# A four-layer fp32 network on one core: five and three tile places, halved opening and ending, and one rounding moved

## The reference

```python
for i in range(2):   # block one
    u = rms_norm(h, g_mix_pre);  gq, gk, gv, gg, ra, aq, ak, av, ga, gb = split(u @ w_in)
    mixed = sigmoid(ga) * (gla(...) @ w_o_gla) + sigmoid(gb) * (attention(...) @ w_o_attn)
    h = h + rms_norm(mixed @ w_out, g_mix_post)
    g, up = split(rms_norm(h, g_ffn_pre) @ w_ffn_in)
    h = h + rms_norm((silu(g) * up) @ w_ffn_out, g_ffn_post)
    h = h + rms_norm(sigmoid(h @ w_ple_gate) * (p @ w_ple_proj), g_ple_post)
for i in range(2):   # block two
    x = x + 0.5 * swiglu(rms_norm(x), ffn1)
    x = x + merged(recurrent, attention) @ w_o
    x = x + 0.5 * swiglu(rms_norm(x), ffn2)
    x = x + sigmoid(rms_norm(x) @ ple_w_gate + b) * (p @ ple_w_proj)
return rms_norm(x, final_norm)
```

## Time and profile before

| | us |
|---|---|
| median of the runs (3) | 2286.14 |
| the profiled execution | 2287.08 |
| its span, first to last instruction | 2285.3 |
| PE busy / DVE busy / ACT busy | 2260.3 / 1577.3 / 1317.1 |
| granted TensorE clock over the span | 0.998 |

### The profile page before, as it was taken

How to read it: one execution, slowest core, us unless ns; L and a number is a source line. 1 busy time by engine, 2 the same in 40 slices (tenths; PEclk the granted TensorE clock), 3 DMA queues, 4 the chain that set the end, 5 groups by cost and what they waited for, 6 DMA issues and landing times.

```text
span 2285.3 us, 31183 instructions
## 1 busy us (share of the span) xinstructions
PE 2260.3 (99%) x13072; PEld 1985.0 (87%) x13072; DVE 1577.3 (69%) x1803; ACT 1317.1 (58%) x1797; POOL 39.0 (2%) x74
## 2 busy tenths in 40 slices
PE   8999999999999999999999999999999999999998
PEld 8898888878988888888898889888888898989886
DVE  6866767478766775667577767675776588667755
ACT  6665655477655655565448745554554558555544
POOL 1000000010000000010000000000100000000000
PEclk9999999999999999999999999999999999999999
DMA  7615555556245655566555355555665655455553
GB/s 227 227 65 184 185 193 188 183 189 231 96 148 184 203 185 193 184 203 193 184 181 178 119 191 191 196 187 186 200 208 177 202 167 166 142 191 183 186 193 120
DMA packets 323515, 411.92 MB, mean 180 GB/s; under 512 B 11600, under 2 KB 245456, under 8 KB 323376
## 3 DMA queue, kind: packets, MB, share of 16 engines
q1 hardware_dynamic: 318160, 394.68, 52.5%
q0 software_dynamic: 4928, 14.26, 2.1%
q10 hardware_dynamic: 288, 0.99, 0.1%
HBM read 408.85 MB, written 1.05 MB: 179 GB/s over the span
## 4 chain that ended last, share of the span: by engine, by line
PE 88%; DVE 5%; ACT 4%; DMA 1%; issue 1%; SPq 0%; DVEq 0%; ACTq 0%
PE banks L610 27%; PE banks L618 14%; PE banks L687 9%; PE banks L689 9%; PE banks L688 9%; PE banks L594 3%; PE banks L595 3%; PE banks L596 3%; DVE lo L1769 2%; ACT hi L1185 1%; DMA raw<-in_w_in 1%; PE banks L738 1%; PE banks L864 1%; PE banks L873 1%; PE banks L841 1%
## 5 line engine op out<-in xcount | busy, mean ns | idle before, releaser
L1769 DVE TENSOR_TENSOR lo<-raw,hi 128x2048 fp32r<-128x2048 f32 (+1 forms) x382 | 858.4, 2250 | 521.9 <-ACT hi L1185 518.0
L1185 ACT ACTIVATE hi<-raw 128x2048 fp32r<-128x2048 f32 (+1 forms) x382 | 715.7, 1878 | 254.3 <-DMA raw<-in_ffn_w_out 84.5
L610 PE MATMUL banks<-x_in,hi 128*128 128x512 f32 x2304 | 537.7, 390 | 0.0
L610 PEld LDWEIGHTS banks<-x_in,hi 128*128 128x128 f32 x2304 | 427.7, 188 | 86.1 <-issue 0.4
L618 PEld LDWEIGHTS banks<-x_in,lo 128*128 128x128 f32 x2304 | 286.5, 192 | 5.8 <-issue 0.2
L618 PE MATMUL banks<-x_in,lo 128*128 128x256 f32 x2304 | 289.3, 283 | 0.0
L594 PE MATMUL banks<-x_in,hi 128*128 128x256 f32 x736 | 210.5, 286 | 0.0
L595 PE MATMUL banks<-x_in,hi 128*128 128x256 f32 x736 | 208.2, 283 | 0.0
L596 PE MATMUL banks<-x_in,lo 128*128 128x256 f32 x736 | 208.2, 283 | 0.0
L687 PE MATMUL banks<-hi,x_hid 128*128 128x512 f32 x528 | 206.0, 390 | 0.0
L689 PE MATMUL banks<-hi,x_hid 128*128 128x512 f32 x528 | 205.5, 389 | 0.0
(11 more groups left out here) (343 smaller groups left out, 3081.0 us busy)
## 6 DMA issues: line engine op xcount, KB each, us to landing
raw<-in_w_in SPq DMA_DIRECT2D x108, 1024.0 KB, 5.1
raw<-in_ffn_w_in SPq DMA_DIRECT2D x88, 1024.0 KB, 5.1
raw<-in_w_ffn_in SPq DMA_DIRECT2D x44, 1024.0 KB, 5.1
raw<-in_ffn_w_out SPq DMA_DIRECT2D x40, 1024.0 KB, 5.1
raw<-in_w_ffn_out SPq DMA_DIRECT2D x20, 1024.0 KB, 5.1
raw<-in_w_o_gla SPq DMA_DIRECT2D x8, 1024.0 KB, 5.2
raw<-in_w_o_attn SPq DMA_DIRECT2D x8, 1024.0 KB, 5.2
raw<-in_w_out SPq DMA_DIRECT2D x8, 1024.0 KB, 5.1
```

What stands on the lines that cost most here:

```text
L610: mm = pe.matmul(bank[b + f], wh[:, k, f * P:(f + 1) * P], x[:, k, :, :].rearrange("p n s -> p (n s)"), start=(start and k == 0), stop=(k ...
L1185: act_fn(high, of, ACT.Copy).then_inc(hi_done.up(), 1)
L1769: tt(rest, of, parts(tile, hi)[0].bitcast(F32), ALU.subtract).then_inc(lo_done.up(), 1)
```

## The change

There are now five places of `raw`/`lo` and three of `hi`. The load of tile n waits for tile n-5, and ScalarE's rounding of tile n gets a wait of its own, for `tile_used` of tile n-3. The first tile is loaded, rounded and subtracted in two halves, the second rounded and subtracted in halves; `opening_rows` takes the place of `rows_in_turn` there and of 40 idle transposes. In the last layer the second 128 tokens of the last projection are done in two column halves, with a chain of halves behind them; the final root is a power on GpSimd, and the output leaves in three DMAs. Four orders differ: block one pumps to `pg[3]` ahead of `turned_high(x_a, 1, 1, 7)`; block two's `pg` stage moves one rounding behind the gates on ScalarE and one behind two `turned_low` on VectorE; VectorE rounds one tile later at `fl`.

```diff
-SLOTS = 4
+SLOTS, HIGHS = 5, 3
@@ pump, ScalarE
                     act.wait_ge(*landed(tile))
+                    if place(tile) >= HIGHS:
+                        act.wait_ge(*tile_used.at(tile.index + 1 - HIGHS))
@@ block one, ScalarE
                 turned_high(x_a, 1, 0, 6)
-                pump(pg[2].index)
+                pump(pg[3].index)
                 turned_high(x_a, 1, 1, 7)
@@ block two, ScalarE, pg
+                pump(pg[3].index)
+                act.wait_ge(*tile_used.at(pg[1].index + 1))
+                for t in range(T):
+                    gate(t, 0)
                 pump(pg[3].index + 1)
-                act.wait_ge(*tile_used.at(pg[1].index + 1))
-                for t in range(T):
-                    gate(t, 0)
@@ block two, VectorE, fl
-                used(BY2["fl"][0])
+                pump(BY2["fl"][0].index + 1)
+                dve.wait_ge(*tile_used.at(BY2["fl"][0].index + 1))
                 tt(fz[:], bank[0][:, 0:S], root_row[:], ALU.mult).then_inc(scaled.up(), 1)
...
+                pump(BY2["fl"][0].index + 2)
@@ block two, VectorE, pg
+                turned_low(x_in, *by_features[0])
+                turned_low(x_in, *by_features[1])
                 pump(pg[3].index + 2)
-                if not last:
-                    turned_low(x_in, *by_features[0])
-                    turned_low(x_in, *by_features[1])
@@ opening, SyncE, ScalarE, TensorE
+                if layer == 0 and tile == TILES1[0]:
+                    sync.dma_start(dst[:, 0:2, :], src[:, 0:2, tile.c0:tile.c0 + tile.nc]).then_inc(first_in.up(), 16)
+                    sync.dma_start(dst[:, 2:4, :],
+                                   src[:, 2:4, tile.c0:tile.c0 + tile.nc]).then_inc(raw_in[slot(tile)].up(), 16)
+                    return
+            first, second = TILES1[:AHEAD]
+            act.wait_ge(*first_in.at(1))
+            high_half(first, 0)
+            turned_high(x_in, *high_turns[0])
+            act.wait_ge(*landed(first))
+            high_half(first, 1)
+            turned_high(x_in, *high_turns[1])
+            act.wait_ge(*x_loaded[0].at(1))
+            norm_tile(0)
+            act.wait_ge(*landed(second))
+            high_half(second, 0)
+            high_half(second, 1)
...
-            idle_turns(40)
-            rows_in_turn(BY1["gva"], x_in, (0, 1), 0, (), *high_turns[2:])
+            opening_rows(BY1["gva"], x_in, (0, 1), *high_turns[2:])
@@ ending, VectorE
+                    ts(xn[:, 0, :], xn[:, 0, :], lroot[:, 0:1], None, ALU.mult).then_inc(xf_ready.up(), 1)
+                    dve.wait_ge(*tile_used.at(pg[3].index + 1))
+                    late_before(1)
+                    dve.wait_ge(*dve_step.now())
+                    late_added(0)
+                    late_times(1)
...
+                    for n in range(2):
+                        cut = slice(n * 512, (n + 1) * 512)
+                        ts(xn[:, 1, cut], xn[:, 1, cut], lroot[:, 1:2], None, ALU.mult).then_inc(xf_ready.up(), 1)
```

More of the change, by code:

```diff
@@ L408, in slot, with high_slot @@
             return place(tile) % SLOTS
+        def high_slot(tile):
+            return place(tile) % HIGHS
         def landed(tile):
@@ L1407, in _, with high_half @@
             warm(ACT.Sqrt)
[L1408 to L1414, removed]
+            def high_half(tile, n):
+                cut = slice(n * TILE // 2, (n + 1) * TILE // 2)
+                act_fn(hi[high_slot(tile)][:, cut], raw[slot(tile)][:, cut],
+                       ACT.Copy).then_inc((hi_done if n else first_hi).up(), 1)
+            first, second = TILES1[:AHEAD]
[10 more added lines that the diff above has]
+            high_half(second, 1)
             act.dma_start(cst[:, P:C_END], dram["consts"][:, P:C_END]).then_inc(const_in.up(), 16)
+            turned_high(x_in, *high_turns[2])
+            turned_high(x_in, *high_turns[3])
+            act.wait_ge(*x_loaded[1].at(1))
+            norm_tile(1)
             for layer in range(DEPTH):
@@ L1728, in _ @@
                     gate(t, 0)
+                pump(pg[3].index + 1)
                 for t in range(T):
@@ L1743, in _ @@
                 for t in range(T):
-                    if t or not last:
-                        act.wait_ge(*h_ready.next())
-                        square(h[:, t, 512:D], hsum[:, t, 1:2])
+                    act.wait_ge(*h_ready.next())
+                    square(h[:, t, 512:D], hsum[:, t, 1:2])
                     root(t, hsum, hbias)
-                    if not last:
-                        turned_high(x_in, *by_features[2 + t])
+                    turned_high(x_in, *by_features[2 + t])
         @block.vector
@@ L1975, in _, with low_half @@
             dve.sem_inc(layer_done.sem, 1)
-            layer_tiles[0] = TILES1[:AHEAD]
-            dve.wait_ge(*first_row.at(1))
[L1978 to L1984, removed]
+            def low_half(tile, n):
+                cut = slice(n * TILE // 2, (n + 1) * TILE // 2)
+                dve.wait_ge(*(hi_done.at(tile.index + 1) if n else first_hi.at(tile.index + 1)))
+                low(lo[slot(tile)][:, cut], raw[slot(tile)][:, cut], hi[high_slot(tile)][:, cut],
+                    lo_done if n else first_lo)
+            first, second = TILES1[:AHEAD]
+            dve.wait_ge(*first_row.at(1))
+            dve.wait_ge(*x_loaded[0].at(1))
+            for n in range(2):
+                with_gain(0, 0, n)
+            low_half(first, 0)
+            turned_low(x_in, *high_turns[0])
+            dve.wait_ge(*x_loaded[1].at(1))
+            with_gain(0, 1, 0)
+            low_half(first, 1)
+            turned_low(x_in, *high_turns[1])
+            with_gain(0, 1, 1)
+            low_half(second, 0)
+            low_half(second, 1)
+            turned_low(x_in, *high_turns[2])
+            turned_low(x_in, *high_turns[3])
             row_served(xn_ready)
@@ L2461, in _ @@
[L2461 to L2464, removed]
+                    gated(t, 1)
+                turned_low(x_in, *by_features[2])
+                turned_low(x_in, *by_features[3])
+                row_served(xn_ready)
+                invert_both()
+                nc.vector.memset(tick[:, 1:2], 0.0).then_inc(layer_done.up(), 1)
         return signals
```

162 lines of the change are left out of this document (127 added, 35 removed).

## The result

| | before | after |
|---|---|---|
| median, us | 2285.70 | 2305.43 |
| span of the profiled execution | 2285.3 | 2303.6 |
| PE busy | 2260.3 | 2264.1 |
| granted TensorE clock over the span | 0.998 | 0.996 |

Both medians are of four executions. The ratio is 1.0087 (95% interval 1.0074 to 1.0099): 19.7 us slower, where 19.9 had been forecast; the two profiled spans differ by 18.3. The four executions of the changed kernel reach from 2302.3 to 2307.3.

The account below looks back on a forecast made before the run. PE, busy 99% of the span, bounds the kernel; -4.2 + 6.6 + 5.5 + 5.8 - 0.1 + 6 + 0.3 = +19.9 on the profiled 2287.08 gives 2307.0, or 2306 beside the median. Range 2291 to 2314.

Parts of the forecast that it names:

- opening: First two tiles: halved loads and roundings let PE finish both at 23.6 instead of 27.8, -4.2 us (bounds 2.5 to 5 gained).
- block one, `pg`, two layers: `ffn1_out` into `pg`: copies of x_a wait behind delayed roundings, PE 0.5 and 2.8 us late per layer, +6.6 in all.
- `va`, two layers: Block two, `ffn1_out` into `va`: rounding of va[1] waits, the last piece comes 2.75 us late per layer, +5.5 in all.
- `ffn2_in`, two layers: Block two, `wo` into `ffn2_in`: rounding 3.6 us later, PE's transpose in by_halves 2.9 late per layer, +5.8 in all.
- the clock: Six new stalls of 2.2 to 2.9 us: five falls to 1.2 GHz at 1.2 each, +6 us (bounds 0 and 10).
- small terms and `pg` stage: `e` 0.4, `wo` of block one 0.6, `fl` -0.6, next transition -0.5, block two's `pg` stage nothing: -0.1 us together.
- ending: After the last matmul: halves and a dropped table load against a later VectorE queue, +0.3 us (bounds -1.5 and +1.5).
- `fl`: At the `fl` tile PE's 1.0 us of waiting should go, but ScalarE's sigmoids and logarithms are late next: 0.6 gained.
- the first rival: The stalls at the new waits leave TensorE's clock alone, so the time is 2300 us; chance 0.22.
- the rival of the lost opening: Without the idle transposes PE has gaps, falls to 1.2 GHz in the first tile, gives the gain back: 2310; chance 0.10.
- the wait moves and nothing is won: Block two's `pg` stage: the moved pump takes the 1.8 us wait from its place, but `xn` comes no earlier; 0 us.
- 1 us later from the site before: Ending: the whole `pg` stage on VectorE runs an estimated 1 us later because of the preceding site.

Follow-up runs that it names:

- covered: The changed kernel with idle transposes put into TensorE's stalls at six places: 2299.84 us, ratio 1.0064 to the kernel before.
- e2: The changed kernel with block one's call as before, pump(pg[2].index) ahead of turned_high(x_a, 1, 1, 7): 2298.03 us, ratio 1.0057.
- e3: The changed kernel with block two's norm_after copying two pieces before its pump and residual adding the last rows before its own: 2286.86 us, ratio 1.0006.
- e6: The kernel before with the halved opening and halved ending alone, four and four places, all four old orders: 2281.15 us, ratio 0.9981.
- e9: The mended orders with four and four places, but ScalarE's order in block two's `pg` stage as in the kernel before: 2283.05 us, one execution.
- e5: The kernel before with five places of raw and three of hi alone; opening, ending and orders as before: 2302.79 us, ratio 1.0073.
- the mended one: The changed kernel, five and three places, with block one's call back at pg[2] and copies first in both blocks: 2280.11 us, ratio 0.9975.
- e4: The changed kernel with 20, 16 and 20 idle transposes ahead of block one's fourth quarter, va[0] and ffn2_in's turned piece: 2299.84 us, ratio 1.0064.
- e1: The changed kernel with four places of raw and four of hi, everything else of the change kept: 2280.84 us, ratio 0.9983.
- e7: The changed kernel, five and three places, with e2's and e3's edits and the first x_a copy ahead of pg[1]'s rounding: 2280.11 us, ratio 0.9975.

## Why the prediction was right, point by point

| term | forecast | measured | from |
|---|---|---|---|
| opening | -4.2 | -3.7 | table, 28 us |
| block one, `pg`, two layers | +6.6 | +7.0 | steps to 474 and to 949 |
| `va`, two layers | +5.5 | +5.7 | 2.8 at 1160, 2.9 at 1813, covered |
| `ffn2_in`, two layers | +5.8 | +5.9 | 3.0 and 2.8 (from 9.91 at 2064), covered |
| the clock | +6 | +5.5 | last row, after less covered |
| small terms and `pg` stage | -0.1 | -1.6 | the rest |
| ending | +0.3 | -0.5 | spans |
| sum | +19.9 | +18.3 | |

"The rest" is 18.8 + 3.7 - 7.0 - 5.7 - 5.9 - 5.5 = -1.6, up to the last row of the table. By the column "covered" it holds -2.0 at the `pg` stage of block two, +0.5 twice at `e` (forecast 0.4 for the two), -0.4 at each of the two places behind block one's `pg` (515 and 970; forecast -0.5 for the two), -0.4 at `fl`, and +0.2 twice elsewhere (up to 935 and up to 2064).

That the sum came so near is in part luck. The terms are off by +0.5 (opening), +0.4 (block one), +0.3 (`va` and `ffn2_in`), -0.5 (clock), -1.5 (small terms) and -0.8 (ending), and these add up to only -1.6. The difference of the medians is nearer still (19.7) because the profiled execution of before, 2287.08, from which the forecast started, was 1.4 above its median.

**The three places.** Each step went as the forecast said, to 0.15 us: 0.61 at the first quarter (forecast 0.5), 2.8 at the fourth (2.8), 2.33 late at `va[0]` (2.2) and 2.8 at the piece behind it (2.75), 3.0 and 2.8 in `ffn2_in` (2.9). What made this possible is that the time of use of every tile can be read from SP's issues in the trace of before, and everything behind the waiting instruction was counted in its queue's order. e2 and e3 took them away one kind at a time, and the gain was what the forecast had put on them or more.

**The clock.** The sum is about right (5.5 for 6), its make-up is not: five falls at 1.2 were taken, there were four new ones at a mean of 1.4, and the old one went. The falls do not go by the length of the stall alone. In the profiled executions of these kernels (us is PE's idle time as the views show it; the steps of the alignment and the lengths in the expectations are up to 0.5 longer):

| stall | us | followed by a fall |
|---|---|---|
| `ffn2_in` | 2.60 | 6 of 6 |
| block one, fourth quarter | 2.54 | 1 of 4 |
| `va[0]` | 2.09 | 2 of 6 |
| `pg` stage, old orders (before, e6) | 1.81, 1.67 | the 1.81 only |
| `pg` stage, e9 | 2.42 | 1 of 1 |

The rows are from before, after and the runs e2, e3, e5, e6 and e9. Each of these falls lasted 3.41 us. Some of what one costs hides: at `va[0]` of layer 2 the matmuls in it take 1.6 longer than in the covered run, but that run then waits 0.57 for `xn`, and 0.8 of the fall's cost is left behind the transposes. That the executions of the changed kernel are spread over 5.0 us and those of the mended one over 0.5 fits a changing number of falls (the shortest has a mean clock of 0.998, the other three 0.996); only one of them has a trace, so this is argued and not shown.

The Trainium skill (TensorE: Matmul & The Clock Gate, HAM oscillation) has as its rule that long idle gaps throttle; its next section (A second HAM failure mode) knows short ones as a repeated pattern between groups of matmuls. Single stalls of 1.81 to 2.60 us are followed by falls here, though not always. By the rule on long gaps the first rival (2300) would have been the time; the covered run, which builds that case, measured 2299.8.

**The opening.** The first half was rounded at 8.31 (forecast 8.1), the second tile at 13.73 (13.5 to 14), PE was through at 24.12 (23.6). The missing 0.5 is there when the second tile's first rows are through (18.66, forecast 18.1), behind PE's stall of 1.07 for that tile's high half; the two quarters behind take the 2.7 each that were forecast. The profile's record of the granted clock starts at 10.0 us in after and at 7.1 in before, with 1.00 in both. Ahead of it PE is slower in after (eight transposes take 1.97 from 7.78 on, where before needs 4.53 for 40), but the first matmul waits for ScalarE's copy and not for them. From 10.0 on the clock stays at 1.00 up to 952 without the 40 idle transposes, so the rival of the lost opening was wrong.

The section of the Trainium skill that the prediction names here (DMA: Bandwidth & Descriptors, Anatomy of one DMA) has its fit from DMAs issued by GpSimd, and these loads are issued by SyncE. For 1024 and 512 KB the formula of that section of the Trainium skill would give 4.4 and 3.2 us (an estimate), where the rows have 5.1 and 3.6; the difference between the two sizes, 1.2 by the formula, is 1.5.

**The steps that failed.** In the `pg` stage of block two the forecast said "the wait moves and nothing is won", since VectorE's chain for `xn` is as long as before. It is as long, but it starts 2.1 us earlier (waits of 2.26 and 0.17 for the gates): I counted VectorE's queue and not what releases its first instruction. This is the -2.0; 0.7 of it is the fall that the kernel before has there and after has not (e6, with the old orders and no fall, steps by -0.7). In the ending the new chain itself was mis-sized. With the orders mended, the last scaling begins 4.19 us behind PE's last matmul, in before 5.04, and the span ends 3.2 behind that, in before 4.3: a gain of 1.9, less 0.4 since PE's last matmul in two column halves comes 0.4 later. The two powers on GpSimd with their hops are in it. The forecast's "1 us later from the site before" is what eats most of it: in after the 4.19 are 5.18, and so they are in the other runs that have five and three places with block two's old `norm_after` (5.20 in e2, 5.19 in e4). With four and four places and the same `norm_after` (e1, e6) they are 4.19, and with five and three and the new one (e3, e7) too. So the delay needs both the waiting rounding and the old order at that site; the chain from there to the ending was not followed. The end of e7:

```profile
2270.61 0.75 DVE L2582 TENSOR_SCALAR xn<-xn,small 128x1024 f32<-128x1024 f32 x1
2270.92 0.28 PE L1231 MATMUL banks<-hi,x_a 128*128 128x256 f32 x1
2271.28 0.48 DVE L2556 SCALAR_TENSOR_TENSOR zt<-banks,small,row 128x256 f32<-128x256 f32 x1
2274.71 0.88 DVE L2599 TENSOR_SCALAR xn<-xn,small 128x512 f32<-128x512 f32 x2 [0.67 <-POOL small L574]
```

Here the scaling of the first 128 tokens is begun before PE's last matmul, and the last half's gate comes 0.36 behind it; in after the scaling is in the way and the gate comes 1.36 behind.

**`fl`.** 0.5 and 0.95 are won, and 0.5 and 0.6 given back some 30 us later (the row of L707 waiting for `lo`, 0.9 at the longest): -0.4 for the forecast's -0.6.

## What to carry to other kernels

Before a buffer count is lowered on an in-order engine, list for each rounding (or other producer) the use that it would wait for and read that time from the trace; wherever it is later than the present start, everything queued behind it moves by the difference, and only the copies that the bound engine needs at once matter. The cure is the order, not the count: with those copies moved ahead of the waiting instruction, five and three and four and four places were within 0.4 us (2280.1 and 2280.5). Price a stall of TensorE of 2 to 3 us with its clock as well (here 1.4 us for each fall, and a fall behind 10 of the 17 stalls of 2.09 to 2.60), and keep idle transposes in mind as a cover where the stall can't be moved.

## What the runs showed of the hardware

- Stalls of the same place and length are followed by a fall of the granted clock in one layer or kernel and not in another; each fall up to the last projection was 3.41 us at 1.2 GHz. What decides it stays open. Idle 128x128 transposes (2.35 us for 20) kept the clock at 1.00.
- A power of one column on GpSimd took 0.55 to 0.56 us, and VectorE was idle for 0.67 us until the scaling could start (the row at 2299.94); the root it replaces was 0.29 on ScalarE and 0.16 on VectorE behind a table load of 1.28.
- Outputs of 256 KB landed 2.2 us after their issue (median), those of 512 KB in before 2.9.
